# Prompt attention of a decoder step: another order of work on TensorE and ScalarE, and the casts of the running sums moved to ScalarE

## What is computed

```python
z = einsum('bqhd,bkhd->bhqk', qb, kb) * scale + bias
mask = kpos[None, :] < qpos[:, None]
log_beta = log_sigmoid(z)
log_keep = where(mask, log_beta - z, 0.0)              # = -log(1 + exp(z)), softplus with its sign turned
rest = cumsum(log_keep, axis=3, reverse=True) - log_keep
a = where(mask, exp(log_beta + rest), 0.0)
out = einsum('bhqk,bkhd->bqhd', a, vb)
```

## The kernel before, in words

| engine | in its loop for step i, in this order |
|---|---|
| PE | scores(i) (or turn), triangles(i-2), values(i-3) |
| ACT | key copies of a turn(i), exponential(i) h 0, 1, weights(i-2) h 0, 1, logarithm(i) h 0, 1, copy of the accumulator if tile i-4 was the last of its half |
| DVE | clamp(i) h 0, 1, sum(i-1) h 0, 1, cast(i-1) h 0, 1, c_lo(i-1) h 0, 1, subtraction of the accumulator if tile i-4 was the last of its half |
| POOL | clears the running sums of the next half (L1415) |
| SP | loads the key rows (L1399) and value rows (L1402) of the next pair |

## Time and profile before

### The profile page before, as it was taken

How to read it: one execution, slowest core, us unless ns; L and a number is a source line. 1 busy time by engine, 2 the same in 40 slices (tenths; PEclk the granted TensorE clock), 3 DMA queues, 4 the chain that set the end, 5 groups by cost and what they waited for, 6 DMA issues and landing times. The chain is left out here.

```text
span 3752.9 us, 57991 instructions
## 1 busy us (share of the span) xinstructions
PE 3221.6 (86%) x20912; PEld 2726.6 (73%) x20912; DVE 1899.9 (51%) x3234; ACT 901.9 (24%) x1502; POOL 610.6 (16%) x528
## 2 busy tenths in 40 slices
PE   5655999999996979788888887888886899999997
PEld 1235999999986979555555554444484899999996
DVE  2566555555543121344444445888824555555554
ACT  0123000000011010333333344666614100000003
POOL 0002122222101111122222221000010222222210
PEclk8887999999998989899999998999998999999998
DMA  8702111111102210788888885000010211111101
GB/s 325 258 26 62 45 45 45 45 40 44 34 0 70 78 60 28 310 351 335 337 340 339 344 345 185 23 17 23 6 45 0 68 45 45 45 45 45 45 22 48
DMA packets 215604, 432.70 MB, mean 115 GB/s; under 512 B 13665, under 2 KB 130058, under 8 KB 212442
## 3 DMA queue, kind: packets, MB, share of 16 engines
q1 hardware_dynamic: 215521, 431.67, 31.6%
HBM read 417.92 MB, written 13.92 MB: 115 GB/s over the span
## 5 line engine op out<-in xcount | busy, mean ns | idle before, releaser
L84 PE MATMUL bank<-hi,mlp_uphi 128*128 128x364 f32 (+1 forms) x1536 | 506.8, 330 | 92.3 <-POOL mlp_uplo L697 92.3
L85 PE MATMUL bank<-lo,mlp_uphi 128*128 128x364 f32 (+1 forms) x1536 | 506.8, 330 | 0.0
L86 PE MATMUL bank<-hi,mlp_uplo 128*128 128x364 f32 (+1 forms) x1536 | 506.5, 330 | 0.0
L85 PE MATMUL bank<-mlp_flo,mlp_dnhi 128*128 128x364 f32 (+1 forms) x1536 | 504.8, 329 | 0.0
L84 PE MATMUL bank<-mlp_fhi,mlp_dnhi 128*128 128x364 f32 (+1 forms) x1536 | 504.7, 329 | 0.0
L86 PE MATMUL bank<-mlp_fhi,mlp_dnlo 128*128 128x364 f32 (+1 forms) x1536 | 504.7, 329 | 0.0
L307 DVE SCALAR_TENSOR_TENSOR x_t<-bank,mod,x_t 128x364 f32<-128x364 f32 (+1 forms) x432 | 245.4, 571 | 379.6 <-PE bank L86 377.3
L84 PEld LDWEIGHTS bank<-hi,mlp_uphi 128*128 128x128 f32 x1536 | 290.4, 189 | 93.4 <-POOL mlp_uplo L697 93.4
L697 POOL TENSOR_TENSOR mlp_uplo<-mlp_raw,mlp_uphi 128x1024 fp32r<-128x1024 f32 x64 | 162.1, 2535 | 825.5 <-ACT mlp_uphi L682 422.7
L85 PEld LDWEIGHTS bank<-lo,mlp_uphi 128*128 128x128 f32 x1536 | 290.5, 189 | 0.0
L86 PEld LDWEIGHTS bank<-hi,mlp_uplo 128*128 128x128 f32 x1536 | 290.4, 189 | 0.0
(11 more groups left out here) (254 smaller groups left out, 5626.8 us busy)
## 6 DMA issues: line engine op xcount, KB each, us to landing
sa_kpage<-in_cache_k SPq DMA_DIRECT2D x256, 512.0 KB, 6.4
sa_vpage<-in_cache_v SPq DMA_DIRECT2D x256, 512.0 KB, 6.0
mlp_raw<-in_w_up SPq DMA_DIRECT2D x64, 512.0 KB, 3.9
mlp_raw<-in_w_down SPq DMA_DIRECT2D x64, 512.0 KB, 3.4
w_raw<-in_w_ada SPq DMA_DIRECT2D x24, 1024.0 KB, 8.6
pm_wada<-in_w_ada SPq DMA_DIRECT2D x48, 512.0 KB, 5.4
kv_raw<-in_w_kv SPq DMA_DIRECT2D x8, 1024.0 KB, 5.6
x_rows<-in_x_prompt SPq DMA_DIRECT2D x1, 4096.0 KB, 13.4
```

Of the source, the lines that this page charges most:

```text
L84: pe.matmul(out, w_hi, x_hi, start=start, stop=False, skip_group_check=True)
L85: pe.matmul(out, w_hi, x_lo, start=False, stop=False, skip_group_check=True)
L86: return pe.matmul(out, w_lo, x_hi, start=False, stop=stop, skip_group_check=True)
```

## The change

- PE: the scores are made one step ahead (`scores(0)` before the loop, then `scores(i + 1)` in step i). The values come one step earlier, values(i-2), and stand behind the scores. The triangles come one step earlier as well, triangles(i-1), and stand last.
- ACT: weights(i-2) and exponential(i) alternate by head (weights h 0, exponential h 0, weights h 1, exponential h 1). Behind them stand the casts of tile i-1 to c_hi for both heads, which DVE did before, then the logarithms of tile i.
- DVE: the two casts are gone; the rest keeps its order. c_lo waits for ACT's cast.
- The buffers and the slots keep their numbers, and no instruction is added or dropped over all: 192 casts go from DVE to ACT.

```diff
--- before.py
+++ after.py
@@ -1422,6 +1422,30 @@
         @block.scalar
         def _(act):
             act.preload_act_table_set("natural_log_exp_and_others")
+
+            def weights(x, h):
+                act.wait_ge(tri_done, 2 * x.n + h + 1)
+                if x.n >= 2:
+                    act.wait_ge(pv_done, x.n - 1)
+                act.activation(att[:, x.n % 2, h, 0:x.w], SLOTS[x.i % 3][h][:, 0:x.w], ACT.Exp).then_inc(att_done, 1)
+
+            def exponential(x, h):
+                act.wait_ge(clamped, 2 * x.n + h + 1)
+                if x.n >= 2:
+                    act.wait_ge(c_done, 2 * (x.n - 2) + h + 1)
+                act.activation(t[:, x.n % 2, h, 0:x.w], SLOTS[x.i % 3][h][:, 0:x.w], ACT.Exp).then_inc(e_done, 1)
+
+            def logarithm(x, h):
+                act.wait_ge(e_done, 2 * x.n + h + 1)
+                act.activation(t[:, x.n % 2, h, 0:x.w], t[:, x.n % 2, h, 0:x.w], ACT.Ln, bias=1.0).then_inc(l_done, 1)
+
+            def high_half(x, h):
+                act.wait_ge(c_done, 2 * x.n + h + 1)
+                if x.n >= 2:
+                    act.wait_ge(tri_done, 2 * (x.n - 2) + h + 1)
+                act.activation(c_hi[:, x.n % 3, h, x.lo:512], c_run[:, x.h % 2, h, x.lo:512], ACT.Copy
+                               ).then_inc(hi_done, 1)
+
             for i in range(N + 5):
                 if i < N and steps[i].turn:
                     x = steps[i]
@@ -1429,24 +1453,18 @@
                         act.wait_ge(turned, 2 * x.pair + h + 1)
                         act.activation(k_t[:, x.pair % 2, 512 * h:512 * h + 512], SLOTS[x.i % 3][h][:, :], ACT.Copy
                                        ).then_inc(k_kept, 1)
-                if x := tile_at(i):
-                    for h in range(2):
-                        act.wait_ge(clamped, 2 * x.n + h + 1)
-                        if x.n >= 2:
-                            act.wait_ge(c_done, 2 * (x.n - 2) + h + 1)
-                        act.activation(t[:, x.n % 2, h, 0:x.w], SLOTS[x.i % 3][h][:, 0:x.w], ACT.Exp).then_inc(e_done, 1)
-                if x := tile_at(i - 2):
-                    for h in range(2):
-                        act.wait_ge(tri_done, 2 * x.n + h + 1)
-                        if x.n >= 2:
-                            act.wait_ge(pv_done, x.n - 1)
-                        act.activation(att[:, x.n % 2, h, 0:x.w], SLOTS[x.i % 3][h][:, 0:x.w], ACT.Exp
-                                       ).then_inc(att_done, 1)
-                if x := tile_at(i):
-                    for h in range(2):
-                        act.wait_ge(e_done, 2 * x.n + h + 1)
-                        act.activation(t[:, x.n % 2, h, 0:x.w], t[:, x.n % 2, h, 0:x.w], ACT.Ln, bias=1.0
-                                       ).then_inc(l_done, 1)
+                now, before, old = tile_at(i), tile_at(i - 1), tile_at(i - 2)
+                for h in range(2):
+                    if old:
+                        weights(old, h)
+                    if now:
+                        exponential(now, h)
+                for h in range(2):
+                    if before:
+                        high_half(before, h)
+                for h in range(2):
+                    if now:
+                        logarithm(now, h)
                 if (x := tile_at(i - 4)) and x.last:
                     act.wait_ge(pv_done, x.n + 1)
                     act.activation(k.hi[:, x.pair, columns(x)], ACC[x.h % 2][:, :], ACT.Copy).then_inc(o_hi, 1)
@@ -1479,11 +1497,6 @@
                             dve.wait_ge(lo_done, 2 * (x.n - 1) + h + 1)
                         dve.tensor_tensor(c, c, t[:, x.n % 2, h, 0:x.w], ALU.add).then_inc(c_done, 1)
                     for h in range(2):
-                        dve.wait_ge(c_done, 2 * x.n + h + 1)
-                        if x.n >= 2:
-                            dve.wait_ge(tri_done, 2 * (x.n - 2) + h + 1)
-                        dve.tensor_copy(c_hi[:, x.n % 3, h, x.lo:512], c_run[:, x.h % 2, h, x.lo:512]).then_inc(hi_done, 1)
-                    for h in range(2):
                         dve.wait_ge(hi_done, 2 * x.n + h + 1)
                         dve.tensor_tensor(c_lo[:, x.n % 3, h, x.lo:512], c_run[:, x.h % 2, h, x.lo:512],
                                           c_hi[:, x.n % 3, h, x.lo:512].bitcast(F32), ALU.subtract).then_inc(lo_done, 1)
@@ -1503,7 +1516,7 @@
                 else:
                     pe.wait_ge(att_done, 2 * before.n + 2)
 
-            for i in range(N + 3):
+            def scores(i):
                 if i < N and steps[i].turn:
                     x = steps[i]
                     pe.wait_ge(k_in, 16 * x.pair + 16)
@@ -1523,7 +1536,22 @@
                                          k.q_t[rows, x.pair, 512 * x.half + x.lo:512 * x.half + 512], start=True,
                                          stop=False, skip_group_check=True)
                     last.then_inc(z_done, 1)
+
+            scores(0)
+            for i in range(N + 3):
+                scores(i + 1)
                 if x := tile_at(i - 2):
+                    pe.wait_ge(att_done, 2 * x.n + 2)
+                    if x.n % 12 == 0:
+                        pe.wait_ge(v_in[x.pair % 2], 16 * (x.pair // 2) + 16)
+                    if x.first and x.h >= 2:
+                        pe.wait_ge(o_kept, x.h - 1)
+                    for h in range(2):
+                        last = pe.matmul(ACC[x.h % 2][64 * h:64 * h + 64, x.lo:512],
+                                         v_rows[x.pair % 2][:, x.j, 64 * h:64 * h + 64], att[:, x.n % 2, h, 0:x.w],
+                                         start=x.first, stop=x.last, skip_group_check=True)
+                    last.then_inc(pv_done, 1)
+                if x := tile_at(i - 1):
                     for h in range(2):
                         z = SLOTS[x.i % 3][h]
                         pe.wait_ge(lo_done, 2 * x.n + h + 1)
@@ -1536,17 +1564,6 @@
                                                  half[:, (x.n - 1) % 3, h, x.lo + x.carry:512], start=False,
                                                  stop=half is c_lo, skip_group_check=True)
                         last.then_inc(tri_done, 1)
-                if x := tile_at(i - 3):
-                    pe.wait_ge(att_done, 2 * x.n + 2)
-                    if x.n % 12 == 0:
-                        pe.wait_ge(v_in[x.pair % 2], 16 * (x.pair // 2) + 16)
-                    if x.first and x.h >= 2:
-                        pe.wait_ge(o_kept, x.h - 1)
-                    for h in range(2):
-                        last = pe.matmul(ACC[x.h % 2][64 * h:64 * h + 64, x.lo:512],
-                                         v_rows[x.pair % 2][:, x.j, 64 * h:64 * h + 64], att[:, x.n % 2, h, 0:x.w],
-                                         start=x.first, stop=x.last, skip_group_check=True)
-                    last.then_inc(pv_done, 1)
```

## The result

The changed kernel takes 3772.0 us, median of 4 executions (3767.3 to 3779.0), against 3753.2 of the kernel before. The ratio is 1.0049, 95% interval 1.0034 to 1.0063: slower by 19 us. Measured a second time, beside the last experiments, it gave 1.0053 (1.0039 to 1.0067). Forecast were 3774, range 3744 to 3796.

The account below looks back on a forecast made before the run. PE's loop through ACT's weights was to replace DVE as the wide-step bound: 48.5 us plus 3.9 detours plus 1.4 low clock, 53.8 a pair, +2.6, +21 for eight, a median of 3774 us (range 3744 to 3796).

Parts of the forecast that it names:

- i: First 512-wide tile after the turn to the next keys: PE's wide loop in full, 4.95 us.
- detours: Places in a pair where another engine is later than PE's loop: 3.9 us added to 48.5.
- d: Fourth tile, 512 wide, last of the first half: 4.49 us in PE's loop.
- g: 384-wide tile of the second half: 3.91 us, plus 0.90 for ACT's accumulator and key copies ahead of its weights.
- e: 128-wide tile that opens the second half: 2.80 us in PE's loop.
- the turn h: 512-wide tile at the turn of the next keys: 5.90 us, plus 1.45 for late triangles behind it.
- j: Second 512-wide tile after the turn: 4.35 us, plus 0.23 for the loop over ACT's cast.
- b: Second tile, 256 wide: 3.00 us, plus 0.38 for the loop over ACT's cast.
- c: Third tile, 384 wide: 3.49 us, plus 0.97 as its weights wait behind ACT's copy and DVE's subtraction.
- the low clock: PE at 1.2 in place of 2.4 GHz, matmuls twice as long: 1.4 us a pair, half of 2.7.
- the first rival: The clock stays up throughout the stage: 52.4 us a pair, +10 us, 3762; chance 0.12.
- The faster one: Detours at two 384-wide tiles and the turn are covered: 49.9 us a pair, 3742, or 3731 at full clock; chance 0.16.

Follow-up runs that it names:

- the change again: The unaltered changed kernel measured once more against the kernel before, beside the last experiments: 3773.6 us, ratio 1.0053.
- values last, copy early: Changed kernel with the values behind the triangles and ACT's accumulator copy ahead of the logarithms, casts still on ACT: 3736.9 us, 0.9948 of the kernel before.

## Why the prediction was right

**The loop.** The step "triangles, weights, scores, values, triangles" is measured link by link above: 4.93 for 4.95 us. That it is the cause is shown by moving the values behind the triangles (0.9994 for 1.0049), by taking PE's order back (0.9987) and by making it alone (1.0050). The full 4.95 is reached in one step of a pair, i. The kernel before has, from triangles to triangles at full clock, d 3.48 to 3.64, g 3.81, i 4.60, j 4.19, k 3.68 and l 3.89 us, so the loop and the detours cost most in d, g, k and l, 0.8 to 1.0 us each; a and e (3.24 before) and the turn h (8.65 before) win back 2.2 us a pair.

**The pair.** Step by step, from triangles to triangles in a pair at full clock (2430.00 to 2482.35), with the predicted figure, detours included, in brackets: a 2.78 (2.80), b 3.40 (3.38), c 4.58 (4.46), d 4.45 (4.49), e 2.78 (2.80), f 3.59 (3.61), g 4.76 (4.81), h 7.39 (7.35), i 4.93 (4.95), j 4.59 (4.58), k 4.44 (4.48), l 4.66 (4.70). The sum is 52.35, predicted 52.4. The largest miss is 0.12 us, in c. Its detour is where it was put (order of time, changed kernel, ACT and DVE at the end of a half; L1470 is the copy, L1505 the subtraction):

```profile
2436.86 0.62 ACT L1470 ACTIVATE hi<-bank 128x512 fp32r<-128x512 f32 x1
...
2437.51 0.69 DVE L1505 TENSOR_TENSOR lo<-bank,hi 128x512 fp32r<-128x512 f32 x1 [0.91 <-ACT hi L1470]
2438.12 0.61 DVE L1486 SCALAR_TENSOR_TENSOR bank<-bank,bias_all,pa_cap 128x128 f32<-128x128 f32 x2
2438.50 0.28 ACT L1436 ACTIVATE pa_t<-bank 128x128 f32<-128x128 f32 x1 [0.65 <-DVE bank L1486]
2438.68 0.48 ACT L1430 ACTIVATE pa_a<-bank 128x384 f32<-128x384 f32 x1
2439.21 0.70 PE L1535 MATMUL bank<-q_t,pa_kt 64*128 64x256 f32 x4 [1.59 <-ACT pa_a L1430]
```

The exponential of e waits 0.65 us for the clamp behind the subtraction, head 1's weights of c come right behind it, and the scores have been idle for 1.59 us.

**The cast.** Taken at 0.60 us, bounds 0.48 and 0.64. Its group in the changed kernel (the last numbers are busy us, mean ns and idle us):

```profile
L1446 ACT ACTIVATE pa_chi<-pa_crun 128x512 fp32r<-128x512 f32 x96 | 57.2, 648 | 0.1
```

It is 0.65 us, just above my upper bound. Since it is not in PE's loop, this cost only the few hundredths of b and j. The Trainium skill, "ScalarE: Activation LUTs", Rules for kernel authors, puts plain work such as add and mul on VectorE; its list does not name casts. The runs agree in part: both casts on ACT alone cost 24 us, both back on DVE gain 5 to 7 us in the change and nothing with the values last and the copy early, and one on each engine is the fastest of all.

**The clock: the term that was off.** I took 1.4 us a pair for the low clock. In the profiled execution it is 0.3 (52.6 less 52.35), in the repeated one 0.8. The pairs of the repeated run, between key loads:

```profile
2348.56:2400.93 52.37, 39.76 (x194) 20.89 (x196) 37.84 (x75) 42.09 (x102) 1.91 (x2) 1.00 0.07 21
2400.93:2455.82 54.89, 42.35 (x194) 22.26 (x196) 37.81 (x75) 42.14 (x102) 1.90 (x2) 0.94 0.07 20
2455.82:2508.19 52.37, 39.78 (x194) 20.90 (x196) 37.83 (x75) 42.08 (x102) 1.91 (x2) 1.00 0.07 21
2508.19:2561.86 53.67, 41.08 (x194) 21.82 (x196) 37.83 (x75) 42.14 (x102) 1.90 (x2) 0.97 0.07 20
```

A pair without any low clock takes 52.37 us, one at 0.97 takes 53.67 and one at 0.94 takes 54.89. The pair at 0.94 has one stay at 1.2 GHz, 6.6 us long (order of time on PE, the change again; the scores of two tiles):

```profile
2441.40 1.23 PE L1535 MATMUL bank<-q_t,pa_kt 64*128 64x256 f32 x4 [1.58 <-ACT pa_a L1430]
...
2448.08 0.92 PE L1535 MATMUL bank<-q_t,pa_kt 64*128 64x384 f32 x4 [0.69 <-ACT pa_a L1430]
```

The scores of 256 columns, 0.70 us in the lines of step c above, take 1.23 here. The stay adds 2.5 us, so a microsecond of low clock costs 0.38, where I had a third. The price was nearly right and the time was too high: I took 4.1 us of low clock a pair, half of 8.2, and the five pairs have 0.7 each in one profiled execution and 2 in the other (estimates from their clocks). In the kernel before, all five pairs show 0.90 to 0.97. In the steady pairs of the change the clock falls in step c or d, behind the 1.59 us that PE is idle in step c, and not in the steps with gaps of 0.7 to 0.9 us. The longest regular gap is thus not the 0.8 us of the prediction but 1.59 in c, and 1.45 at the turns. With few such gaps the clock falls less often than before, as the second half of my argument had it and as the first rival put it in full. I had named a mean clock above 0.97 as a sign against the forecast; it came in one profiled execution (0.99) and not in the other (0.96).

**The sum.** 52.6 less 51.2 is 1.4 a pair, 11 us for eight, and the profiled execution was 12.6 us longer than that of before (3767.3 and 3754.7). The repeated one has 53.1 us a pair, 15 us for eight, and was 18 us longer (3772.7). Its first pair, which I had not treated apart, ran at the low clock to about 2338.7 us (to about 2325.7 in the first execution) and took 56.2 us from triangles to triangles, against 51.3. My +21 us were 10 for the loop and its detours and 11 for the clock. Measured are 9 for the loop (52.35 less 51.2 in eight pairs), and for the clock 2 to 6 in the pairs and up to 5 in the first pair. The mechanism of the +10 was right; that the total came within 2 us of the median of 3772 is luck, since the clock's term was too high and stood in part for the start of the stage.

**Signs.** DVE below 320 us and ACT near 350 in the stage came (302 and 336). That PE's wait in weight loads would go far above 90 us did not: it is 91.6. The wait is in the row of the matmuls, 76.0 us in place of 37.9, 86 times for 55. The triangles' wait for c_lo fell in that row from 22.6 us to 14.8 and hardly in the row of weight loads, from 67.6 to 64.0. c_lo's wait for the cast, 80.8 us, I had not listed.

**The rivals.** The faster one, with the detours covered, fell: c, g and the turn all cost what was written. The cast as the main cause fell for the change as a whole (5 to 7 us of 19), but holds for the cast alone in the old order (24 us).

## What to carry to other kernels

When stages of a pipeline are pulled a step ahead, write the order of each engine beside what each block waits for, and look for a block directly behind the one that starts its input's chain: the latency of the round trip over another engine is then idle time in every step, however little each engine has to do. The same three blocks in another order (values behind the triangles) took 20 us off. A combined change should be measured part by part: here one part was worth -18 us, one +19, one +24 alone and 5 to 7 in company. The best two kernels, at 0.9915 and 0.9926, take the good part, have the values behind the triangles, split the casts between two engines, and move ACT's copy ahead of the logarithms, which was no part of the change.

## What the runs showed that was not expected

A cast of 128x512 from SBUF to SBUF in fp32r takes 648 ns on ACT and 419 ns on DVE, and yet moving both to ACT changed the total by 0 us (values last, copy early), by 5 to 7 (in the change), by 14 (with the alternation, PE's order of before) or by 24 (alone), and moving one of them by -15 (0.9915 for 0.9954), according to what stood behind it, which no busy time tells. One kernel's executions spread by 12 to 17 us: 3767 to 3779 for the change, 3746 to 3763 for the kernel before in its largest group, 23 executions. The low clock differs from execution to execution (five pairs of the change at 0.97 to 1.00, then at 0.94 to 1.00), but that this is the whole of the spread was not tested.
